# Queries and keys of the second attention turned by on-chip transfers and VectorE blocks instead of TensorE transposes

## What is computed

```python
def _rope(x):                      # x: (1, 256, heads, 128)
    x1, x2 = xf[..., :half], xf[..., half:]
    return jnp.concatenate([x1 * cos - x2 * sin, x2 * cos + x1 * sin], axis=-1)

proj = h @ w_in[l]                 # queries, keys, values of two attentions, 8 heads of 128 each
qa, ka, va = ...; qb, kb, vb = ...
ya = _moba_attention(_rope(qa), _rope(ka), va) @ w_moba_out[l]
yb = _dsa_attention(_rope(qb), _rope(kb), vb, q_idx, k_idx, p_wi) @ w_dsa_out[l]
y = (sigmoid(ga) * ya + sigmoid(gb) * yb) @ w_o[l]
# then a residual, and f = square(relu(h @ w_ff1)) @ w_ff2 with another residual
```

## Time and profile before

| | |
|---|---|
| median of 3 runs | 1786.38 us (1786.08 to 1786.91) |
| time of the profiled execution | 1786.64 us |
| its span, first to last instruction | 1785.0 us |
| PE busy (matmuls) | 1769.9 us, 99% |
| DVE busy | 1259.2 us, 71% |
| ACT busy | 895.0 us, 50% |
| granted TensorE clock, mean | 0.999 |
| groups of the second attention | about 410 to 736 us of the span |

### The profile page before, as it was taken

How to read it: one execution, slowest core, us unless ns; L and a number is a source line. 1 busy time by engine, 2 the same in 40 slices (tenths; PEclk the granted TensorE clock), 3 DMA queues, 4 the chain that set the end, 5 groups by cost and what they waited for, 6 DMA issues and landing times.

```text
span 1785.0 us, 25525 instructions
## 1 busy us (share of the span) xinstructions
PE 1769.9 (99%) x8242; PEld 1454.6 (81%) x8242; DVE 1259.2 (71%) x1691; ACT 895.0 (50%) x1267; POOL 124.1 (7%) x217
## 2 busy tenths in 40 slices
PE   8999999999999999999999999999999999999998
PEld 7777778887888888888888888888888888888886
DVE  5677779778877867787777868777775654545545
ACT  6866675555445454544444545444444444444443
POOL 1011101010000000110010101000000000000000
PEclk9999999999999999999999999999999999999999
DMA  9778788655667778699999966999998775655554
GB/s 348 253 262 283 240 278 313 203 183 181 205 214 253 237 221 286 204 317 318 304 305 303 317 211 224 327 311 318 311 293 240 235 222 191 196 190 194 193 190 140
DMA packets 195053, 446.93 MB, mean 250 GB/s; under 512 B 17088, under 2 KB 27312, under 8 KB 194608
## 3 DMA queue, kind: packets, MB, share of 16 engines
q1 hardware_dynamic: 166544, 342.23, 58.9%
q0 software_dynamic: 28304, 103.89, 17.4%
q10 hardware_dynamic: 144, 0.03, 0.0%
HBM read 434.03 MB, written 12.06 MB: 250 GB/s over the span
## 4 chain that ended last, share of the span: by engine, by line
PE 95%; DMA 2%; DVE 1%; ACT 1%; SPq 0%; issue 0%; DVEq 0%; ACTq 0%
PE bank L1579 30%; PE bank L1581 30%; PE bank L1580 30%; DMA raw<-in_w_in_a 2%; PE bank L1625 1%; PE bank L1749 1%; PE bank L1732 1%; DVE w_lo L1001 0%; PE bank L1724 0%; PE bank L1842 0%; PE bank L1848 0%; PE bank L1721 0%; DVE x L1028 0%; PE bank L1605 0%; ACT y L594 0%; PE bank L1854 0%
## 5 line engine op out<-in xcount | busy, mean ns | idle before, releaser
L1001 DVE TENSOR_TENSOR w_lo<-raw,w_hi 128x1024 fp32r<-128x1024 f32 x605 | 728.8, 1210 | 412.2 <-ACT w_hi L590 409.9
L590 ACT ACTIVATE w_hi<-raw 128x1024 fp32r<-128x1024 f32 x605 | 633.5, 1050 | 712.0 <-PE bank L1581 644.1
L1579 PE MATMUL bank<-w_hi,h_hi 128*128 128x512 f32 x2272 | 896.2, 394 | 3.7 <-DVE w_lo L1001 2.4
L1581 PE MATMUL bank<-w_hi,h_lo 128*128 128x512 f32 x2272 | 885.8, 390 | 0.0
L1580 PE MATMUL bank<-w_lo,h_hi 128*128 128x512 f32 x2272 | 885.1, 390 | 0.0
L1579 PEld LDWEIGHTS bank<-w_hi,h_hi 128*128 128x128 f32 x2272 | 426.9, 188 | 95.8 <-issue 5.3
L1581 PEld LDWEIGHTS bank<-w_hi,h_lo 128*128 128x128 f32 x2272 | 426.6, 188 | 89.8
L1580 PEld LDWEIGHTS bank<-w_lo,h_hi 128*128 128x128 f32 x2272 | 427.1, 188 | 85.2
L515 POOL DMA_DIRECT2D ada_raw<-in_w_ada x160 | 84.7, 530 | 953.1 <-DVE acc_a L1008 709.8
L1008 DVE SCALAR_TENSOR_TENSOR acc_a<-ada_raw,cond,acc_a 128x1024 f32<-128x1024 f32 x112 | 143.3, 1280 | 10.8 <-DMA ada_raw<-in_w_ada 10.7
L1008 DVE SCALAR_TENSOR_TENSOR acc_b<-ada_raw,cond,acc_b 128x1024 f32<-128x1024 f32 x48 | 64.3, 1340 | 1.5 <-DMA ada_raw<-in_w_ada 1.4
(11 more groups left out here) (209 smaller groups left out, 934.6 us busy)
## 6 DMA issues: line engine op xcount, KB each, us to landing
raw<-in_w_ff SPq DMA_DIRECT2D x256, 512.0 KB, 4.7
raw<-in_w_in SPq DMA_DIRECT2D x176, 512.0 KB, 4.6
ada_raw<-in_w_ada POOLq DMA_DIRECT2D x160, 512.0 KB, 5.5
raw<-in_w_in_a SPq DMA_DIRECT2D x69, 512.0 KB, 5.0
ada_more<-in_w_ada POOLq DMA_DIRECT2D x32, 512.0 KB, 5.7
raw<-in_w_out_a SPq DMA_DIRECT2D x32, 512.0 KB, 5.6
raw<-in_w_o SPq DMA_DIRECT2D x32, 512.0 KB, 5.2
raw<-in_w_moba SPq DMA_DIRECT2D x16, 512.0 KB, 5.6
```

Of the source, the lines that this page charges most:

```text
L590: act.activation(used(w_hi, turn, s), used(raw, turn, s), ACT.Copy).then_inc(hi_ready, 1)
L1001: dve.tensor_tensor(used(w_lo, turn, s), used(raw, turn, s), used(w_hi, turn, s).bitcast(F32), ALU.subtract).then_inc(lo_ready, 1)
L1579: pe.matmul(out_ap, hi, rhs_hi, start=start, stop=False)
L1581: return pe.matmul(out_ap, lo, rhs_hi, start=False, stop=stop)
```

## The change

The rotation's last two instructions per token block write `rot` in another order of columns (`rot_by_quad`), so that what has to end on one quadrant of 32 partitions lies together. Then 16 transfers per rotation, each of 32 partitions by 256 columns (32 KB), carry `rot` to `rope_ab`, quadrant i to quadrant j (`move_rot`). They are issued by SP between the weight loads, in four portions j of 4 transfers: after the loads of units 6 and 7 of the following turn, and of units 0 and 1 of the turn after it. DVE turns the 32x32 blocks with two `transpose` instructions of 512 columns per rotation into `q2_t` or `k2_t` (`turn_qk`), after its split in step s = 6. The eight times 8 transposes of PE and the eight times 2 copies of ACT fall away. `rope_ab` is the two scratch tiles of the rotation, at the same place as before, and so each rotation now waits until the one before has been turned (`qk_ready`); SP waits for `rot_ready` before the first portion. SP's loop over these turns is written out.

```diff
@@ -16,6 +16,7 @@
 QUADS = P // QUAD
+MOVES = 16 * QUADS * QUADS
 UNIT = KG * CH
@@ -167,8 +168,7 @@
             with ExitStack() as a2:
-                rope_a = sb("rope_a", [P, CH], on=a2)
-                rope_b = sb("rope_b", [P, CH], on=a2)
+                rope_ab = sb("rope_ab", [P, T * CH], on=a2)
                 rot = sb("rot", [P, T, CH], on=a2)
@@ -197,6 +197,8 @@
         y_home = nc.dram_tensor("y_home", (CHUNKS - 1, P, T * CH), F32, kind="Internal").ap()
+        rope_a, rope_b = rope_ab[:, 0:CH], rope_ab[:, CH:2 * CH]
+        rot_flat = rot[:, :, :].rearrange("p t n -> p (t n)")
         f_blk = acc_b[:, T * CH:2 * T * CH]
@@ -295,7 +297,7 @@
         mask_ready = sem("mask_ready")
-        qk_turned = sem("qk_turned")
+        rot_moved = sem("rot_moved")
         qk_ready = sem("qk_ready")
@@ -428,12 +430,27 @@
                 load(TURN_KI, s, w_2[:, k:k + KG, col:col + cols])
-            for half in range(2):
-                with sp.Fori(0, 2) as b:
-                    for part in range(3):
-                        load_chunk((b + 2 * half) * 3 + TURN_GRP + part, w_2,
-                                   b * CH + (half * 3 + part) * W2)
-            load_chunk(TURN_GATE, w_2, COL_GA)
+            def move_rot(n, j):
+                if j == 0:
+                    sp.wait_ge(rot_ready, (n + 4) * T)
+                    if n:
+                        sp.wait_ge(qk_ready, n * T)
+                part = slice(j * T * P, (j + 1) * T * P)
+                for i in range(QUADS):
+                    sp.dma_start(rope_ab[j * QUAD:(j + 1) * QUAD, i * T * P:(i + 1) * T * P],
+                                 rot_flat[i * QUAD:(i + 1) * QUAD, part]).then_inc(rot_moved, 16)
+            def load_with_rot(turn, col, late=None, early=None):
+                for s in range(UPT):
+                    load(turn, s, w_2[:, KG * s:KG * s + KG, col:col + CH])
+                    if s >= UPT - 2 and late is not None:
+                        move_rot(late, s - UPT + 2)
+                    if s < 2 and early is not None:
+                        move_rot(early, s + 2)
+            for g in range(4):
+                for part in range(3):
+                    load_with_rot(g * 3 + TURN_GRP + part, g % 2 * CH + (g // 2 * 3 + part) * W2,
+                                  (None, 2 * g, 2 * g + 1)[part], (2 * g - 1 if g else None, None, 2 * g)[part])
+            load_with_rot(TURN_GATE, COL_GA, None, 7)
             load_chunk(TURN_GATE + 1, w_2, COL_GB)
@@ -849,11 +866,6 @@
                         act.sem_inc(evicted[PAIR_B][t], 1)
-            def keep_qk(n, dst):
-                for t in range(T):
-                    act.wait_ge(qk_turned, n * T + t + 1)
-                    act.activation(dst[:, :, t * P:t * P + P], two(banks[TURNED + t][:, :], 4), ACT.Copy)\
-                        .then_inc(qk_ready, 1)
             def attn2(g, k):
@@ -871,12 +883,8 @@
                     split(g * 3 + TURN_GRP + 1, s + AHEAD)
-                    if s == 4:
-                        keep_qk(g * 2, q2_t)
                 for s in range(UPT):
                     split(g * 3 + TURN_GRP + 2, s + AHEAD)
-                    if s == 4:
-                        keep_qk(g * 2 + 1, k2_t)
                 for t in range(T):
@@ -1290,7 +1298,7 @@
             residual_turn(1, TURN_QI - 1, PAIR_A, (7, 6), y1)
-            def rope(src, dst, stepped, use, t, n, heads, half, cos0, sin0, copies=1):
+            def rope(src, rows, stepped, use, t, n, heads, half, cos0, sin0, copies=1):
                 cols = heads * 2 * half
@@ -1307,11 +1315,9 @@
                 dve.wait_ge(stepped, use + 1)
-                rows = dst.rearrange("p (h r d) -> p h r d", h=heads * copies, r=2)
                 for c in range(copies):
                     for r in range(2):
-                        ins = dve.tensor_tensor(rows[:, c * heads:(c + 1) * heads, r, :], ra[:, :, r, :], rb[:, :, r, :],
-                                                (ALU.subtract, ALU.add)[r])
+                        ins = dve.tensor_tensor(rows(c, r), ra[:, :, r, :], rb[:, :, r, :], (ALU.subtract, ALU.add)[r])
                 ins.then_inc(rot_ready, 1)
@@ -1336,7 +1342,8 @@
                 chunk_result(t, turn, turn)
-                rope(pair[PAIR_A][t][:, :], rot[:, t, :], evicted[PAIR_A][t], 7 + n // 2, t, n, CH // IDX_DIM,
+                rows = rot[:, t, :].rearrange("p (h r d) -> p h r d", h=CH // IDX_DIM, r=2)
+                rope(pair[PAIR_A][t][:, :], lambda c, r: rows[:, :, r, :], evicted[PAIR_A][t], 7 + n // 2, t, n, CH // IDX_DIM,
                      IDX_DIM // 2, C_COSI, C_SINI)
@@ -1347,15 +1354,24 @@
                     .then_inc(w_idx_ready, 1)
-                rope(ki[:, 0:IDX_DIM], rot_key[:, t, :], ki_roped, t, t, 1, 1, IDX_DIM // 2, C_COSI, C_SINI, 2)
+                rows = rot_key[:, t, :].rearrange("p (h r d) -> p h r d", h=2, r=2)
+                rope(ki[:, 0:IDX_DIM], lambda c, r: rows[:, c:c + 1, r, :], ki_roped, t, t, 1, 1, IDX_DIM // 2, C_COSI,
+                     C_SINI, 2)
             dve.wait_ge(i_turned, T)
             for t in range(T):
                 rope_index(TURN_QI_2, t)
             dve.wait_ge(w_idx_ready, T)
+            rot_by_quad = rot_flat.rearrange("p (r e t h d) -> p t r h e d", r=2, e=2, t=T, h=4)
             def rope_chunk(p, turn, use, n):
                 for t in range(T):
                     chunk_result(t, turn, turn)
-                    rope(pair[p][t][:, :], rot[:, t, :], evicted[p][t], use, t, n, 4, DH_2 // 2, C_COS, C_SIN)
+                    rope(pair[p][t][:, :], lambda c, r: rot_by_quad[:, t, r], evicted[p][t], use, t, n, 4, DH_2 // 2,
+                         C_COS, C_SIN)
+            back = rope_ab[:, :].rearrange("p (i t h d) -> p t h i d", i=QUADS, t=T, h=4)
+            def turn_qk(g, n, dst):
+                dve.wait_ge(rot_moved, g * (2 * MOVES) + (n + 1) * MOVES)
+                for t in range(T):
+                    dve.transpose(dst[:, :, t * P:(t + 1) * P], back[:, t]).then_inc(qk_ready, 1)
             def attn2_norm(g, k):
@@ -1390,7 +1406,7 @@
                 else:
-                    dve.wait_ge(qk_turned, g * 2 * T)
+                    dve.wait_ge(qk_ready, g * 2 * T)
                 rope_chunk(PAIR_B, g * 3 + TURN_GRP, g * 2 + 7, g * 2 + 3)
@@ -1399,7 +1415,9 @@
                         ada(g * 10 + 56, 2 + s // 2, acc_a, g * 5 - 3 + s // 4)
-                dve.wait_ge(qk_turned, g * 2 * T + T)
+                    if s == 6:
+                        turn_qk(g, 0, q2_t)
+                dve.wait_ge(qk_ready, g * 2 * T + T)
                 rope_chunk(PAIR_A, g * 3 + TURN_GRP + 1, g + 9, g * 2 + 4)
@@ -1410,6 +1428,8 @@
                         ada(g * 10 + 56, 6 + s // 2, acc_a, g * 5 - 1 + s // 4)
+                    if s == 6:
+                        turn_qk(g, 1, k2_t)
             def attn2_turn(g, turn, m=None, k=0):
@@ -1826,10 +1846,6 @@
             turn_key()
-            def turn_qk(n):
-                for t in range(T):
-                    pe.wait_ge(rot_ready, (n + 3) * T + t + 1)
-                    turn_rows(rot, t, 4, banks[TURNED + t], qk_turned)
             def attn2(g, k):
@@ -1857,13 +1873,8 @@
                     chunk_unit(g * 3 + TURN_GRP + 1, s, PAIR_A, g + 9)
-                    if s == 3:
-                        pe.wait_ge(o2_kept, g * 4 + 1)
-                        turn_qk(g * 2)
                 for s in range(UPT):
                     chunk_unit(g * 3 + TURN_GRP + 2, s, PAIR_B, g * 2 + 8)
-                    if s == 3:
-                        turn_qk(g * 2 + 1)
             def attn2_turn(g, turn, p, use):```

The order of the instructions shows the three places. `ISA` and `REGISTER_ALU` rows are register and wait instructions.

PE before, in the keys' or values' turn of a group g > 0 (the loop's body): end of unit 3, the 8 transposes, start of unit 4.

```order
L1581 MATMUL bank<-w_hi,h_lo 128x512
L1861 ISA
L1831 ISA
L1625 MATMUL bank<-consts,rot 128x128 x4
L1831 REGISTER_ALU
L1625 MATMUL bank<-consts,rot 128x128 x4
L1590 REGISTER_ALU
L1579 MATMUL bank<-w_hi,h_hi 128x512
```

## The result

The changed kernel is slower: 1804.68 us, the median of four runs (1803.1 to 1807.68), against 1786.56 us before. The ratio is 1.0104, 95% interval 1.0086 to 1.0121. Its profiled execution took 1803.1 us, with a span of 1801.0 us where the span before was 1785.0. So 16.0 us of span are to be found, on top of the 7.0 us that were to come off.

A forecast was written before the change was run, and what follows sets the result against it. The prediction took PE's instruction list plus its waits as the bound. Transposes -7.0 and a group 0 wait +0.5 gave -6.5 us, hence 1779.9 us (forecast band 1778.4 to 1782.7, chance 0.72; range 1777.8 to 1784.5, 0.82).

The forecast's parts named there:

- What bounds the kernel: Whole kernel: PE's instruction list plus its waits; new PE waits only through `w_lo`, by DVE or a late load.
- PE's transposes: PE's 64 transposes in 8 blocks: 0.88 us each from start to start, 7.0 us less.
- the duration reading: Rival on PE: each transpose worth its full duration, 64 x 0.272 = 17.4 us less, 1769 us; chance 0.01.
- the rotation's two last instructions: DVE's rotation writing pieces of 32 columns, not 64: cost 0, bounds 1.7 us at T17.3 and 13.5 in all.
- DVE's block transposes: Two per rotation behind DVE's split in step 6: 711 ns each, cost 0 in groups 1 to 3.
- SP's issues: SP's transfers between weight loads: 0.4 us each, 1.6 a portion, 6.4 a rotation; cost 0, with little left.
- T21.1's load 0.8 late: Group 1, behind the third portion: this load 0.8 us later than 525.70, covered by the room at T21.3.
- Landing: The 32 KB transfers into `rope_ab`: 4.9 us, up to 8.5, in time for DVE's block transposes.
- Group 0: First group, without room: late load and DVE make PE wait 0.5 us at T18.3, bounds 0 and 1.5.
- issues are slow: Rival on SP: at 1.07 us an issue the loads run late, +41 us, 1828; chance 0.08 for above 1790.
- DVE's hold: Rival on DVE: late last portion or loads eat the gain, 1783 to 1787; chance 0.14 shared with dearer rotation.
- a dearer rotation: Rival on DVE: the new column order costs 0 to 13.5 us; chance 0.14 shared with DVE's hold.

The follow-up runs named there:

- run 1: The changed kernel without its 128 on-chip transfers, everything else kept (second attention's numbers not the reference's): 1780.11 us, ratio 0.9963.
- run 10: The changed kernel without its 128 transfers, timed once more in another set: 1779.45 us.
- run 6: The changed kernel with the same 128 transfers in size and shape, read from the input in HBM and not from `rot` in SBUF: 1789.63 us, ratio 1.0017.
- run 2: The changed kernel with its 128 transfers cut from 256 columns to 8 (1 KB each in place of 32 KB): 1797.17 us, ratio 1.0058.
- run 8: The changed kernel with 8 transfers of 512 columns per rotation in place of 16 of 256, same bytes, wrong columns: 1786.20 us, ratio 1.0002.
- run 4: The changed kernel with two of each portion's four transfers issued by ACT and two by SP, same bytes and number: 1784.62 us, ratio 0.9990.
- run 9: The changed kernel with 8 transfers per rotation on SP, 4 on ACT, 4 replaced by ACT copies, values copied before ACT's last rounding: 1780.56 us, ratio 0.9966.

## Why the prediction was wrong

It expected 1779.9 us, 6.5 less than before; the kernel came out 18 us slower. By its own steps:

- *What bounds the kernel*: right, but incomplete in the ways to a wait. The bound was PE's list plus its waits, and the new waits came by the way named there, "a late load ahead of ACT and DVE". But that list named `w_lo` as the only door. The second one, a PSUM bank that ACT has yet to empty because its list is stuck at a late load, was missed, and 8.5 us came through it.
- *PE's transposes*, 8 x 0.88 = 7.0: right. Runs 1 and 10 gave 7.0 and 6.4. The measure from start to start held, and the duration reading (17.4) did not.
- *ACT's copies* 0 and *the rotation's two last instructions* 0: right. Line 1320 has the 422 ns of before (415/422/427), with writes in pieces of 32 columns.
- *DVE's block transposes*: right, a little cheap: 686 ns instead of 711, without any idle time ahead of them for `rot_moved`. Run 1 shows that they fit into the slack.
- *SP's issues*: **this step failed.** It took 0.35 to 0.4 us an issue, 1.6 a portion, and found "cost 0, but with little left". The issue measured 0.59, the portion 2.4 to 2.5, and the load behind it 0.58 where it took 0.37. The row taken had the shape but another source. By run 6 the source makes most of the difference: 422 ns out of HBM, 590 out of SBUF (the 348 of the row taken is not reached even so). The row that did read SBUF (1.07 us) was put aside as being of another size and shape, and runs 2 and 8 show that size is nothing to an issue here (1 to 64 KB). The value lay between the two rows, and I took one of the ends. The step found a cost of 0; the runs put it at 17 us or more of a loss of 25 (run 2 against run 1).
- *T21.1's load 0.8 late* followed from that. By issues of 0.59 the third portion ends 8.7 us after the rotation (522.82 to 531.5), not 5.6, and the lateness grows with each load. T21.2's, which the keys' rotation stands behind, was not followed at all.
- *Landing*: right. 3.7 us at the median, at most 5.2 (taken 4.9, up to 8.5). DVE was never held by `rot_moved`. The figure quoted beside it, from the Trainium skill, "DMA: Bandwidth & Descriptors", Anatomy of one DMA, is given there for transfers that GpSimd issues. Here SyncE issued them, and the estimated 2.1 us for 32 KB compares with 1.8 at the least and 3.7 at the median.
- *Group 0*, 0.5 at T18.3: place right, size 1.4, within its bounds (0 to 1.5), for the same cause.
- The rival *issues are slow* had the mechanism and the sign, with 0.08. Its price was built on 1.07. Its threshold, "starts to cost from about 0.6", was reckoned with the last portion's landing, a limit that never came into force. The loads between the portions set the real one: four issues and a load against PE's unit of 2.8 us. At 0.42 an issue that step is 2.37 us and the moves cost about 10 us (run 6 against run 1); at 0.59 it is 3.1 and they cost 25. So it starts to cost below 0.42, and outweighs the 7 us from somewhere below 0.42 too, not from 0.8. *DVE's hold* and *a dearer rotation* did not happen.
- The clock was in no step: 6 us came from it, behind three of the seven waits.

The Trainium skill, "DMA: Bandwidth & Descriptors", Issuing engines are not separate DMA queues, says that issuing from several engines saves only the sequencer's time, which is usually small beside the transfer. The runs agree with both: run 4 saves time on SP's sequencer, and an issue of 0.59 us is small beside a landing of 3.7. But that small time was the main cause here, since the same queue feeds a stream that wants a load every 2.8 us: runs 4 and 8 took half of it from SP and got back 20 and 18 us.

What stays open: the split of the 7.5 us between run 2 and the change (bytes ahead of the loads, or the clock); what decides whether a wait costs clock; what holds SP for 590 ns on an SBUF source; and which part of run 9 gave its last 2.5 us.

## What to carry to other kernels

Price a transfer by what it costs the queue that issues it, from a row with the same source and destination memories, not of the same size: a queue that also feeds a stream has a budget per unit, here 2.8 us, and 4 issues and a load of 0.59 each are over it. When a stream gets late, look on each engine for what stands behind its wait in program order: here a rotation on DVE and a copy out of PSUM on ACT carried the delay to PE, and three of the seven waits, of 1.9 to 3.5 us, cost clock as well. Issuing half of the moves from an engine with free time, taking the values' copy out from behind a late load, and a plain copy for what stays in its partitions made a loss of 18 us into a gain of 5 (run 9). Fewer and larger moves gave nearly as much as the first of these (run 8), in a kernel that moved the wrong columns.

## What was not expected of the hardware

- SP's issue took 590 ns at the median for 1 KB, 32 KB and 64 KB alike from SBUF to SBUF, and 422 ns from HBM to SBUF at the same 32 KB; on ACT 608 ns. A weight load right behind such issues took 0.58 us instead of 0.37, behind those out of HBM 0.42. So an issue's time hangs on what was issued just before it, too: the first of a portion, behind a load, took 0.51 at the median.
- PE's unit took 5.3 us at a granted clock of 0.50 behind one wait of 3.5 us. The clock fell behind waits of 2.24 and 1.91 us too, and stayed at 1.00 behind others of 2.72 and 1.96.
- The 32x32 block transpose of 128x512 float32 took 667 to 708 ns on DVE, the same tile of another stage 711.
